# A two-layer decoder trunk: attention scores in two row halves of the array, three passes of 64 rows

## What is computed

```python
# layer 0: differential attention, 4 heads, two maps of width 64 each, values of width 128
s = einsum('bqmhd,bkmhd->bmhqk', q, k) * dk ** -0.5 - slopes * dist   # masked to dist >= 0
p = softmax(s);  a = p[:, 0] - lam * p[:, 1];  y = a @ v
# layer 1: 8 heads of width 64, three branches (window, dilation) with softmax weights between them
s = q @ k * dh ** -0.5 - slopes * dist                                # masked to the branch
```

## Time and profile before

| | |
|---|---|
| median of 3 executions | 2178.66 us (2177.98 to 2179.24) |
| profiled execution | 2180.61 us, span 2178.8 us |
| TensorE busy | 2131.6 us, 98% of the span |
| VectorE, ScalarE, GpSimd busy | 1316.2, 901.0, 864.7 us |
| scores, product, turning in layer 0 | from 212 to about 345 us |
| the same in layer 1 | from about 1312 to 1444 us |
| granted TensorE clock | 0.999 of full speed, 2.4 GHz |

### The profile page before, as it was taken

How to read it: one execution, slowest core, us unless ns; L and a number is a source line. 1 busy time by engine, 2 the same in 40 slices (tenths; PEclk the granted TensorE clock), 3 DMA queues, 4 the chain that set the end, 5 groups by cost and what they waited for, 6 DMA issues and landing times.

```text
span 2178.8 us, 30055 instructions
## 1 busy us (share of the span) xinstructions
PE 2131.6 (98%) x10572; PEld 1775.4 (81%) x10572; DVE 1316.2 (60%) x1725; ACT 901.0 (41%) x1497; POOL 864.7 (40%) x571
## 2 busy tenths in 40 slices
PE   8999899999999999999999998899999999999999
PEld 7877798888888887888888887778888888887887
DVE  4345875775565555458597346666865555555555
ACT  4134874443333333345333147752433333334433
POOL 1022432467667763002164024320576667751000
PEclk9999999999999999999999999999999999999999
DMA  5021321055554557676302120311255554557565
GB/s 192 1 58 49 126 79 30 20 171 195 196 186 156 166 174 258 199 242 189 116 20 59 59 68 21 121 55 39 68 193 193 194 174 157 170 179 274 193 193 193
DMA packets 229534, 295.55 MB, mean 136 GB/s; under 512 B 11824, under 2 KB 133168, under 8 KB 229168
## 3 DMA queue, kind: packets, MB, share of 16 engines
q1 hardware_dynamic: 229136, 294.04, 41.6%
q10 hardware_dynamic: 288, 0.05, 0.0%
HBM read 208.06 MB, written 77.59 MB: 131 GB/s over the span
## 4 chain that ended last, share of the span: by engine, by line
PE 78%; issue 13%; DVE 3%; ACT 3%; POOL 2%; DMA 1%; SPq 0%; POOLq 0%; DVEq 0%; ACTq 0%
PE PS L1592 12%; PE PS L1590 12%; PE PS L1591 12%; PE PS L1617 6%; PE PS L1618 6%; PE PS L1619 6%; PE PS L1119 4%; PE PS L1121 4%; PE PS L1120 4%; PE PS L1203 2%; POOL QRS L1009 1%; PE PS L1173 1%; PE PS L1309 1%; PE PS L1308 1%; PE PS L1307 1%
## 5 line engine op out<-in xcount | busy, mean ns | idle before, releaser
L2198 DVE TENSOR_TENSOR LINEl<-LINE,HIGH 128x1024 fp32r<-128x1024 f32 x154 | 194.0, 1267 | 170.6 <-ACT HIGH L1648 170.2
L1648 ACT ACTIVATE HIGH<-LINE 128x1024 fp32r<-128x1024 f32 x154 | 163.2, 1060 | 238.2 <-PE PS L1619 216.9
L1617 PE MATMUL PS<-HIGH 128*128 128x512 f32 x616 | 240.8, 391 | 4.8 <-ACT KEEP L1648 4.4
L1619 PE MATMUL PS<-HIGH,LINEl 128*128 128x512 f32 x616 | 240.4, 390 | 0.0
L1618 PE MATMUL PS<-LINEl,HIGH 128*128 128x512 f32 x616 | 240.3, 390 | 0.0
L2198 DVE TENSOR_TENSOR SLOTl<-BLOCKS,RING 128x512 fp32r<-128x512 f32 x168 | 153.6, 914 | 94.3 <-ACT RING L1648 89.5
L941 POOL TENSOR_TENSOR ST<-ST 128x512 f32<-128x512 f32 x132 | 192.1, 1455 | 33.4 <-DMA ST<-in_ffn_w_down 24.8
L1648 ACT ACTIVATE RING<-BLOCKS 128x512 fp32r<-128x512 f32 x168 | 105.9, 631 | 227.8 <-PE PS L1592 213.2
L2198 DVE TENSOR_TENSOR SLOTl<-SLOT,RING 128x512 fp32r<-128x512 f32 x126 | 135.2, 1073 | 87.0 <-ACT RING L1648 86.8
L1617 PEld LDWEIGHTS PS<-HIGH 128*128 128x128 f32 x616 | 116.1, 188 | 30.1 <-issue 5.2
L1009 POOL TENSOR_TENSOR QRS<-QMS,EXPO 128x8 f32<-128x8 f32 x32 | 52.1, 1638 | 220.7 <-DVE QMS L2459 220.1
(11 more groups left out here) (426 smaller groups left out, 5712.9 us busy)
## 6 DMA issues: line engine op xcount, KB each, us to landing
LINE<-hidden SPq DMA_DIRECT2D x154, 256.0 KB, 2.8
hidden<-HID SPq DMA_DIRECT2D x44, 512.0 KB, 4.3
ST<-in_ffn_w_down SPq DMA_DIRECT2D x44, 512.0 KB, 4.1
sums<-ST SPq DMA_DIRECT2D x22, 1024.0 KB, 6.2
hidden<-ST SPq DMA_DIRECT2D x22, 1024.0 KB, 6.7
LINE<-sums SPq DMA_DIRECT2D x88, 256.0 KB, 3.0
BLOCKS<-in_ffn_w_gate SPq DMA_DIRECT2D x42, 512.0 KB, 4.0
BLOCKS<-in_ffn_w_up SPq DMA_DIRECT2D x42, 512.0 KB, 5.3
```

The source lines that it names most:

```text
L1617: pe.matmul(dst, hi[:, 0, ts], hi[:, 1, :], start=j == 0 and not adds_on, stop=False, skip_group_check=adds_on)
L1619: pe.matmul(dst, lo[:, 0, ts], hi[:, 1, :], start=False, stop=j == NJ - 1, skip_group_check=adds_on).then_inc(dn_pe, 1)
L1648: return nc.scalar.activation(dst, src, ACT.Copy, **kw)
L2198: return v.tensor_tensor(dst, src, hi.bitcast(F32), ALU.subtract)
```

## The change

The stacks go. `factors_of(u)` gives four tiles of a unit, keys high and low (KH, KL), queries high and low (QH, QL), each 128 partitions by 1024, map A in rows 0 to 63 and map B in 64 to 127, as in QK. A chunk of scores takes three passes of 64 rows for each map, high·high, high·low and low·high; the two maps stand side by side in the instruction stream, A on rows 0 to 63, B on rows 64 to 127, into their own banks. ScalarE and GpSimd make a factor in one instruction over 128 partitions, two per unit, in rounds 1 and 3. The exchanging DMAs and their semaphore are gone. `scores` waits for both maps' s_mx.

In layer 0 S of both maps now stands ahead of W. In layer 1 S of both maps stands behind T of A, ahead of W and T of B. Layer 1's bias tables alternate between two sets (BX and BIAS) and are made in rounds 1 and 3 of the unit before.

```diff
+        def stack(k, u):
+            hi, lo = factors_of(u)[2 * k:2 * k + 2]
+            return QK[:, (UNITS + u, u)[k], :], hi[:], lo[:]
...
-            def score(L, m, b, g, i):
-                pe.wait_ge(s_mx[m][L], g + i + 1)
+            def scores(L, g, i):
                 u, t = (g + i) // NT, (g + i) % NT
-                keys = P * (t + 1)
+                kh, kl, qh, ql = factors_of(u)
+                keys, qs = P * (t + 1), slice(P * t, P * t + P)
+                for m in range(2):
+                    pe.wait_ge(s_mx[m][L], g + i + 1)
                 for c0 in range(0, keys, HALF):
                     c1 = min(keys, c0 + HALF)
-                    q, dst = queries_of(u, L)[m][:, P * t:P * t + P], PS[:, 1024 * m + c0:1024 * m + c1]
-                    pe.matmul(dst, q, keys_of(u)[0][m][:, c0:c1], start=True, stop=False)
-                    last = pe.matmul(dst, q, keys_of(u)[1][m][:, c0:c1], start=False, stop=True)
-                last.then_inc(s_pe[m][L], 1)
+                    for k, (q, key) in enumerate(((qh, kh), (qh, kl), (ql, kh))):
+                        for m in range(2):
+                            own = slice(HD * m, HD * m + HD)
+                            last = pe.matmul(PS[:, 1024 * m + c0:1024 * m + c1], q[own, qs], key[own, c0:c1], start=k == 0, stop=k == 2)
+                            if c1 == keys and k == 2:
+                                last.then_inc(s_pe[m][L], 1)
...
 # layer 0, TensorE
-                            if more:
-                                score(0, 0, b, g, i + 2)
+                            if u + 1 < UNITS or i < NT - 2:
+                                scores(0, g, i + 2)
                             if g + i > 0:
                                 weigh(g + i - 1)
-                            if more:
-                                score(0, 1, b, g, i + 2)
...
 # layer 1, TensorE
                             turn(1, 0, u, i)
-                            if more:
-                                score(1, 0, b, g, i + 2)
+                            if u + 1 < UNITS or i < NT - 2:
+                                scores(1, g, i + 2)
                             if g + i > 0 and i % 2 == 0:
                                 weigh_unit(g + i - 2)
                                 weigh_unit(g + i - 1)
...
                             turn(1, 1, u, i)
-                            if more:
-                                score(1, 1, b, g, i + 2)
...
 # layer 1, VectorE
-                            dve.wait_ge(s_mx[m][1], g + 9)
+                            dve.wait_ge(s_mx[m][1], g + 1)
                             bias(m, 1 - b, 2 * u + 2 + m)
...
-                        if i == NT - 2 and u + 1 < UNITS:
+                        if i == 1 and u + 1 < UNITS:
                             next_bias(0)
...
-                        if i == NT - 2 and u + 1 < UNITS:
+                        if i == 3 and u + 1 < UNITS:
                             next_bias(1)
```

More of the change, by code:

```diff
@@ L271, in small, with factors_at @@
             return t
[L276 to L281, removed]
+        def factors_at(tag, o):
+            return tuple(at(f"{name}{tag}", [P, TOK], F32R, o + 4 * KB * k) for k, name in enumerate(("KH", "KL", "QH", "QL")))
+        FIRST = factors_at("X", oX)
+        LATER = [factors_at(str(b), oHH + 16 * KB * b) for b in range(2)]
+        BX = [at(f"BX{m}", [P, TOK], F32, oX + (24 + 4 * m) * KB) for m in range(2)]
         BIAS = [at(f"BIAS{m}", [P, TOK], F32, oHL + 4 * KB * m) for m in range(2)]
@@ L355, in trunk @@
         stack_hi, stack_lo = sem("stack_hi"), sem("stack_lo")
-        staged = sems("staged")
         x_out = sem("x_out")
@@ L408, in trunk @@
         GU_AT = (0, GU + 7 * 5)
[L411 to L417, removed]
+        STACKS = 2
+        STACK_AT = tuple(L * UNITS * STACKS for L in range(3))
         TILES0 = NT * UNITS
@@ L426, in stacks_before, with factors_of @@
         def stacks_before(L, u):
[L428 to L448, removed]
+            return STACK_AT[L] + STACKS * u
+        def factors_of(u):
+            return LATER[u % 2] if u else FIRST
+        def stack(k, u):
+            hi, lo = factors_of(u)[2 * k:2 * k + 2]
+            return QK[:, (UNITS + u, u)[k], :], hi[:], lo[:]
         WV_LO = ((1, 2), (4, 6))
@@ L696, in _ @@
                 for u in range(UNITS):
[L697 to L702, removed]
                     if u == (1, 3)[L]:
@@ L1376, in _ @@
                         qk_turn(0, 7)
-                pe.wait_ge(staged[0], 128 * L + 64)
-                pe.wait_ge(stack_lo, STACK_AT[L] + 4)
+                pe.wait_ge(stack_lo, STACK_AT[L] + STACKS)
                 pe.wait_ge(bank_free[L], 2 * NT + 3)
-                for m in range(2):
-                    score(L, m, 0, 0, 0)
+                scores(L, 0, 0)
                 qk_turn(1, 5)
                 qk_turn(1, 6)
-                for m in range(2):
-                    score(L, m, 0, 0, 1)
+                scores(L, 0, 1)
                 qk_turn(1, 7)
@@ L1472, in _ @@
                             turn(1, 1, u, i)
-                            if i == NT - 2 and more:
-                                pe.wait_ge(stack_lo, following + 4)
-                            if more:
-                                score(1, 1, b, g, i + 2)
                     weigh_unit(TILES0 - 2)
@@ L1873, in _ @@
                             act.wait_ge(x_out, 16 * NT)
-                        for step in STACK0:
-                            stack_high(step, 0, 0)
+                        for k in range(STACKS):
+                            stack_high(k, 0)
                         if L == 0:
@@ L1913, in split_o @@
                     copy(OUT_W[1][g % 2][0][:], (RD if g else WO1s)[:]).then_inc(wo_hi, 1)
-                def next_stack(g, b, u, *ks):
-                    for k in ks:
-                        if STACK[k][0] is QST and u > 1:
-                            m, first = STACK[k][1], STACK[k][2] == 0
-                            act.wait_ge(s_pe[m][L], g if L else g + (2 if first else NT))
-                        stack_high(STACK[k], b, u)
                 def turned(m, g, i):
```

94 lines of the change are left out of this document (34 added, 60 removed).

## The result

The changed kernel takes 2211.3 us, median of 4 runs (2201.35 to 2216.39); the kernel before, measured beside it, 2178.5. The ratio of the record is 1.014, 95% interval [1.0121, 1.0159] (the two medians alone stand as 1.015): slower by 1.4%, where 2193 us (0.7%) was forecast. Two things are in that: some 20 us that every run has, and up to 15 us that differ from run to run.

The account below looks back on a forecast made before the run. TensorE was taken to bound layer 0 (VectorE its first unit), the order of waits layer 1. The profiled 2180.61 us, -5 for layer 0 and +19 for layer 1, made 2194.6; 1.95 lower for the median, 2193 us; eight-in-ten range 2173 to 2220.

Parts of the forecast that it names:

- Part 5: Layer 1, both maps' scores ahead of the product with V: each round becomes one chain through VectorE, +19 us.
- The walk: Layer 1's chain added round by round: starts of map B's turnings, with the next unit at 37.0 us instead of 31.8.
- partly serial pairs: Rival: the row halves overlap only in part, at 0.3 of the serial cost; up to 2209 us, chance 0.06.
- Part 4: Layer 0, scores ahead of the product with V: output projection covers the wait; layer 0 saves 5 us.
- Part 1: Scores as three half-row passes: a 512-column pair runs side by side in 0.23 us, saving 1.7 us per unit.
- Part 2: Entering and leaving the array's halves: 0.1 us per change, net 0.12 a round, 1 us lost per unit.
- Part 3: Split copies over 128 rows: per unit some 5.4 us less on GpSimd and 2.5 on ScalarE; fewer held combines.
- The tables in Part 5: Layer 1's bias tables, made in rounds 1 and 3, run under the scores, freeing two places in round 6.
- Serial pairs: Rival: the two row halves run one after the other, 5.8 us more in each of eight units; 2239 us, chance 0.15.
- Layer 1 not one chain: Rival: TensorE's work, not the wait for VectorE's map B pass, sets layer 1's round; 2166 us, chance 0.08.
- half of it: Rival: in layer 1 only map B's VectorE pass is waited for, 5 to 8 us; 2174 to 2183, chance 0.10.
- turning point: Layer 1, round 5: whether VectorE's bias passes end within map A's turning, 0.7 us; the rows said 2.5.

Follow-up runs that it names:

- e2: The changed kernel with layer 1's paired scores moved behind the turning of map B, last in the round; 2180.5 us.
- e1: The kernel before, 128-row stacks kept, with only the new order: both maps' scores together where map A's stood, in both layers; 2195.4 us.
- e7: The changed kernel with layer 1's bias tables for the next unit made in round 6 again instead of rounds 1 and 3; 2215.8 us.
- e5: The changed kernel with unused identity turnings as filling ahead of the scores in rounds 1 to 3 of layer 0's first unit; 2202.7 us.
- e10: The changed kernel with layer 1's paired scores last in the round and identity turnings as filling in layer 0's first unit; 2175.6 us.
- e8: The kernel before, 128-row stacks, with layer 1's scores of both maps moved behind the turning of map B; 2170.4 us.
- e6: The changed kernel, layer 1's pairs last; in layer 0's first unit half-row scores by map, A ahead of the product with V, B behind; 2195.1 us.
- e3: The changed kernel with layer 1's scores in half rows, one map at a time, at the places of the kernel before; 2207.0 us.
- e9: The kernel before, 128 rows, with layer 0's scores together ahead of the product, layer 1's last, and filling in layer 0's first unit; 2170.4 us.
- e12: The kernel before with layer 1's scores last and three 128-row passes a chunk instead of two in layer 0's first unit; 2170.7 us.

## Why the prediction was wrong, point by point

- **Direction and the main mechanism: right.** Part 5 forecast +19 us for layer 1 from a chain through bA and bB; it is 20.5, a unit 37.55 for 37.0. The walk came true round by round, too: in the third unit the turnings of B start 2.8, 6.8, 10.6, 15.7, 20.6, 27.9, 30.6 and 37.6 us from round 0, each at most 0.6 behind the forecast. e2 undoes the place and takes 25 us away. e1 splits it: 13.7 come with the order and 6.8 more with the pairs and the early tables together. As the tables save 1.2 us in each of three units (e7), the pairs by themselves probably cost more than 6.8, most likely because they tie both maps together; that reason is read from the code and has no run of its own. Only the waits were put too high: some 40 us expected, 29.7 measured.
- **The step that failed: the clock isn't in the sum.** The groups by stage show 1.00 throughout, and the sum took that over, without a word, for a kernel in which TensorE was forecast to stand far longer and to work on half rows. From the profiled run to the median the clock costs some 10 us, and 2 in layer 0 of the profiled run (133.7 against 131.6 in e5). At full clock the kernel takes 2199 us (e5's two runs), 6 over the forecast; the other 12 of the 18 us are the clock's. With them the result lies above the forecast's own 2184 to 2207 us, and inside the wider 2173 to 2220 only because that left room for partly serial pairs, which did not come. The 6 us at full clock are, as near as they can be told, layer 0's 5.8 (Part 4: a saving forecast that did not come) and layer 1's 1.5, less 2.6 that the rest of the program gained unforeseen, and 2 more because the forecast put the median that much under the profiled run.
- **Part 1: right.** A pair of 512 every 0.23 us, 0.23 taken; in layer 1's records the second matmul of a pair starts under 0.04 us after the first, as forecast (under 0.1). The estimate of 0.30 from the Trainium skill's row packing ("TensorE: Matmul & The Clock Gate", Part 3) was for four tiles and doesn't hold for these two halves of 64.
- **Part 2: mis-sized, 0.12 us a round taken, 0.31 measured** (the earlier trace rows against the timeline above). The change into the halves takes 0.23 us in the round of 896 columns: the last O matmul holds the pair back by 0.12 and the first pair by 0.11 (0.34 instead of 0.23). The change back takes 0.19: the last pair lasts 0.27 instead of 0.17, and in the records the second V matmul starts 0.21 us after the first instead of 0.11. So a change costs 0.2, not 0.1. A turning straight behind W adds 0.08, which is the order's: in e1, with 128 rows, W lasts 0.89 us, in the kernel before 0.81, in the kernel after 1.00 (the same round of the second unit, e1 first):

```profile
265.19 1.05 PE L1215 MATMUL PS<-V,PT 128*128 128x128 f32 x8
266.08 0.60 PE L1203 MATMUL PS<-IDN,PR 128*128 128x128 f32 x4
```

```profile
266.46 1.16 PE L1185 MATMUL PS<-V,PT 128*128 128x128 f32 x8
267.45 0.71 PE L1173 MATMUL PS<-IDN,PR 128*128 128x128 f32 x5
```

  Against that go one late pair of scores (298.03 to 298.34, where the text has two a round; those at 296.40 are not late), 0.07 ahead of the turning, and 0.04 in it. That eats the 0.40 that this round saves but for 0.09. At 0.31 a round it is 2.5 us a unit for the 1.0 taken; the bound of 0.27 per change allowed 2.7 on top of that, and is not reached.
- **Part 3: partly wrong.** The copies shrank as said (KL 2.41 us for 128 rows), but held combines stayed. GpSimd, free sooner, begins QWl (a low part that it makes in both kernels) at 294.29 instead of 295.78 and now meets the combine of 512 columns; before it met the next one (640 columns, 1.92 us), and TensorE did not wait for that. The wait of 0.75 us shown above is the only one of its kind in the wide units, and layer 0's third unit is 0.8 us longer than before (34.30 against 33.53), as in e5 and e10.
- **Part 4: wrong by 5.8 us.** Layer 0 was to save 5. At full clock it costs 0.8 us (e5, 131.6 against 130.9): the first unit saves 0.2 for 1.2 forecast, the second nothing, the third loses the 0.8 of the held combine. With 128 rows the order saves 0.5 us in each of the two units in the middle (e1); the halves' changes (Part 2) take that and the saved passes.
- **The tables in Part 5: right in kind.** 1.2 us a unit (e7).
- **Rivals.** Serial pairs: no. Layer 1 not one chain, or half of it: no. Their turning point, whether bA and bB end behind T(A), is what e2 moves: with the scores last they end mostly in time (6.0 us of waits are left).

**Open.** What makes the clock fall, in full. Waits have a part in it (e5 fills them, and the fall at 220 us is gone), but the clock of e8 fell with no wait over 0.7 us in the 4 us ahead of it, and that of e10 ahead of its filling. In e6 64-row passes by map went with 44 us at the lower level, and in e3's layer 1 such passes, without waits, left the clock at 1.00. Nor were pairs tried in layer 0 with the product between them, since a pair can't be split.

## What to carry to other kernels

Ask of every moved wait two things: which other engine's chain it closes, and what the clock does while TensorE stands. Here moving the same scores from one place in the round to another was worth 25 us, while the pairs themselves lost 2 to 3 us a layer against full rows; try the place first, and leave between an answer's request and its use the work that can cover it. When a kernel's runs spread more than those of its predecessor, look at the mean clock of each run before anything in the program.

## What the runs showed of the hardware

- Two matmuls of 64 rows in the two row halves run fully side by side at fp32r (a pair of 512 columns every 0.23 us), but going into the halves and coming back cost 0.2 us each (kernel after, layer 0), and three such passes lost to two of 128 rows by 1.9 us in layer 0 (e5, e9) and 2.9 in layer 1 (e2, e8).
- A TensorE that is busy all the time can stay at 1.2 GHz: 44 us in e6, with 64-row passes by map. As many passes on 128 rows ran at 2.4 GHz there (e12), and 64-row passes by map did in layer 1 (e3).
- Waits of 1.4 to 2.2 us were followed in some executions, and not in others, by a fall of the clock to 1.2 GHz, for 3.5 us in layer 1 (1.5 us lost each) and up to 14 in layer 0 (e2). Shorter waits, of 1.1 us at most, were also followed by one (e8, e10).
- A turning straight behind the fp32r matmuls of W starts 0.08 us later than scores do there (e1, 0.89 us from W's start against 0.81 before).
- A VectorE combine of 512 columns took 0.98 us alone and 2.33 beside a GpSimd subtraction (before and after).
